# Transformer layer, attention heads: queries projected with their weights stationary and rotated transposed; keys and values token by token, two tiles to a PSUM bank

## The reference

```
h = rms_norm(x);  z = h @ w_in            # columns: pool | q1|q2 | k1|k2 | v | gates
q, k: 8 heads x (2 x 64); rotary on the first 16 of each 64;  v: 8 heads x 128
attn = (softmax(q1 k1) - lambda softmax(q2 k2)) @ v   # block-causal mask by chunks of 64
```

## Time and profile before

| | us |
|---|---|
| median of three runs (845.28 to 847.25) | 845.69 |
| span of the profiled execution | 843.6 |
| heads: from the first projection to the last | 120 to 338 |

### The profile page before, as it was taken

One profiled execution on the slowest core, in us unless ns is written; L12 is line 12 of the kernel. 1 busy time (PEld: TensorE's weight loads), 2 busy tenths in 40 slices (PEclk: granted clock), 3 DMA queues, 4 the chain that ended last, 5 costly groups with the idle time before them and its releaser, 6 DMA issues.

```text
span 843.6 us, 15839 instructions
## 1 busy us (share of the span) xinstructions
PE 821.1 (97%) x5378; PEld 748.1 (89%) x5378; DVE 588.7 (70%) x957; ACT 512.7 (61%) x935; POOL 87.6 (10%) x76
## 2 busy tenths in 40 slices
PE   8999999999999999999999999999999999999992
PEld 7999999999999999999999888888888888888881
DVE  6373332777677768467467126999989999989995
ACT  7343313666566656565525233488888887888884
POOL 0000000000000000000000001222223322223112
PEclk9999999999999999999999999999999999999996
DMA  9632213232133213332234746699999999999925
GB/s 274 139 103 83 67 44 95 82 109 75 36 104 107 59 54 108 102 101 75 79 123 157 270 177 204 236 371 372 380 377 374 368 368 367 364 368 367 351 70 193
DMA packets 135959, 163.54 MB, mean 194 GB/s; under 512 B 18599, under 2 KB 103719, under 8 KB 135914
## 3 DMA queue, kind: packets, MB, share of 16 engines
q1 hardware_dynamic: 129674, 149.53, 52.7%
q0 software_dynamic: 5952, 12.82, 5.4%
q10 hardware_dynamic: 288, 0.59, 0.2%
HBM read 151.61 MB, written 20.12 MB: 204 GB/s over the span
## 4 chain that ended last, share of the span: by engine, by line
PE 52%; DVE 3%; DMA 2%; issue 1%; ACT 1%; POOLq 0%; POOL 0%; ACTq 0%
PE ps L1748 15%; PE ps L1750 15%; PE ps L1749 15%; PE ps L2182 2%; PE ps L2094 1%; DMA xg<-sum_rows,idi 1%; PE ps L2101 1%; PE ps L2204 1%; DMA sum_rows<-yb,ydn 1%; PE ps L2086 0%; PE ps L2127 0%; PE ps L2128 0%; PE ps L2025 0%; DVE wl L1144 0%; PE ps L1953 0%
## 5 line engine op out<-in xcount | busy, mean ns | idle before, releaser
L1623 DVE TENSOR_TENSOR wl<-rawM,wh 128x1024 fp32r<-128x1024 f32 x189 | 223.9, 1220 | 14.3 <-ACT wh L980 12.4
L980 ACT ACTIVATE wh<-rawM 128x1024 fp32r<-128x1024 f32 x192 | 195.8, 1057 | 6.2 <-PE ps L1750 2.8
L1748 PE MATMUL ps<-hTh,wh 128*128 128x272 f32 (+2 forms) x448 | 131.0, 292 | 1.4 <-ACT qkv L804 1.0
L1750 PE MATMUL ps<-hTh,wl 128*128 128x272 f32 (+2 forms) x448 | 129.5, 289 | 0.0
L1749 PE MATMUL ps<-hTl,wh 128*128 128x272 f32 (+2 forms) x448 | 128.9, 288 | 0.0
L1748 PE MATMUL ps<-wh,xh 128*128 128x256 f32 (+1 forms) x384 | 124.3, 324 | 0.3 <-DVE xl L1669 0.3
L1750 PE MATMUL ps<-wh,xl 128*128 128x256 f32 (+1 forms) x384 | 121.7, 317 | 0.0
L1749 PE MATMUL ps<-wl,xh 128*128 128x256 f32 (+1 forms) x384 | 121.6, 317 | 0.0
L1748 PE MATMUL ps<-wh,hTh 128*128 128x384 f32 x256 | 90.0, 352 | 0.2 <-DVE mA L1254 0.2
L1748 PEld LDWEIGHTS ps<-hTh,wh 128*128 128x128 f32 x448 | 84.3, 188 | 3.0 <-ACT qkv L804 1.3
L1750 PE MATMUL ps<-wh,hTl 128*128 128x384 f32 x256 | 86.3, 337 | 0.0
(11 more groups left out here) (324 smaller groups left out, 1711.5 us busy)
## 6 DMA issues: line engine op xcount, KB each, us to landing
rawM<-in_w_expert_up SPq DMA_DIRECT2D x64, 512.0 KB, 9.2
rawM<-in_w_expert_down SPq DMA_DIRECT2D x64, 512.0 KB, 8.0
rawM<-in_w_expert_gate SPq DMA_DIRECT2D x64, 512.0 KB
rawA<-in_w_in SPq DMA_DIRECT2D x64, 192.0 KB, 3.0
rawA<-in_w_in SPq DMA_DIRECT2D x20, 512.0 KB, 5.3
rawA<-in_w_attn_branch SPq DMA_DIRECT2D x8, 512.0 KB, 3.5
rawA<-in_w_out SPq DMA_DIRECT2D x8, 512.0 KB, 4.2
x<-in_x_prompt SPq DMA_DIRECT2D x4, 512.0 KB, 6.7
```

Source lines behind the costliest of these rows:

```text
L980: nc.scalar.activation(wh[:, (c + 1) % S, :], rawM[:, slot, :], ACT.Copy).then_inc(m_hi, 1)
L1623: V.tensor_tensor(wl[:, sl, :], rawM[:, slot, :], wh[:, sl, :].bitcast(F32), ALU.subtract).then_inc(m_lo, 1)
L1748: T.matmul(out, sh, mh_, start=start, stop=False, **kw)
L1750: return T.matmul(out, sl, mh_, start=False, stop=stop, **kw)
```

## The change

Queries are no longer part of the token-by-token projection. For each step j a new `queries(j, half)` holds the 128 query columns of the weights stationary and streams 272 tokens past them, twice, into banks 3 and 4: the queries come out transposed. Keys and values keep their form, with 256 streamed columns instead of 384; tiles 0 and 1 share bank 0, tiles 2 and 3 bank 1, tile 4 has bank 2. So ACT evacuates three times (512, 512 and 256 columns) instead of five (384 each), and `acc_mm` is given after tiles 1 and 3. In steps 0 to 6 the queries come after the tiles, in step 7 ahead of them.

DVE rotates the queries in the transposed layout: `read_queries` multiplies both banks by a table of cosines and swaps the halves by a stream shuffle, `turn_queries` multiplies by a table of sines and adds. Both tables (128 x 544) are loaded once. `turn` makes six transposes (keys only), and the high part of the queries is made from SBUF.

```diff
             def evacuate(h, banks=range(NEV)):
+                for b in banks:
+                    if b < 2:
+                        act.wait_ge(acc_mm, 2 * h + b + 1)
...
             def attend(g, nxt, early=None, last=False):      # ACT
-                act.wait_ge(acc_ev, NT * (g + 1))
+                act.wait_ge(q_done, g + 1)
+                nc.scalar.activation(qh[:], q_turned[:], ACT.Copy).then_inc(q_hi, 1)
+                act.wait_ge(acc_ev, NEV * (g + 1))
...
             def join_sample(g):
-                dve.wait_ge(acc_ev, NT * (g + 1))
-                V.tensor_tensor(qkv[LAST:P, 4, :], ps[2 * DEC:LAST, 4, 0:384], qkv[LAST:P, 4, :],
+                dve.wait_ge(acc_ev, NEV * (g + 1))
+                V.tensor_tensor(kv[LAST:P, 4, :], ps[2 * DEC:LAST, 2, 0:KV], kv[LAST:P, 4, :],
                                 ALU.add).then_inc(dec_done, 1)
+            def read_queries(g, lk):
+                dve.wait_ge(q_mm, g + 1)
+                V.tensor_tensor(two(q_turned[:]), halves, two(q_cos[:]), ALU.mult)
+                V.stream_shuffle(two(q_swap[:]), halves, HALF_SWAP).then_inc(q_free, 1)
+            def turn_queries(g, lk):
+                dve.wait_ge(q_free, g + 1)
+                lk(V.tensor_tensor(q_swap[:], q_swap[:], q_sin[:], ALU.mult))
+                V.tensor_tensor(q_turned[:], q_turned[:], q_swap[:], ALU.add).then_inc(q_done, 1)
...
             def attend(g, nxt, lk, last=False):              # DVE
+                dve.wait_ge(q_hi, g + 1)
+                V.tensor_tensor(ql[:], q_turned[:], qh[:].bitcast(F32), ALU.subtract)
                 dve.wait_ge(tr_hi, 2 * g + 1)
-                V.tensor_tensor(ql[:, 0:SEQ], ps[:, 5, :], qh[:, 0:SEQ].bitcast(F32), ALU.subtract)
...
             DVE's pass, head(h)
+                read_queries(h - 1, lk)
                 if not first:
                     probs(h - 2, 2, lk)
+                turn_queries(h - 1, lk)
                 join_sample(h - 1)
+                rope(h - 1, lk)
                 if not first:
                     probs_lo(h - 2, 2)
-                rope(h - 1, lk)
...
             def project(h, j, after={}):
+                if j == KD - 1:
+                    queries(j, 0, sl, q0)
+                    queries(j, 1, sl, q0).then_inc(q_mm, 1)
                 for t in range(NT):
-                    if j == 0:
-                        pe.wait_ge(acc_ev, NT * (h - 1) + t + 1)
+                    if j == 0 and t % 2 == 0:
+                        pe.wait_ge(acc_ev, NEV * (h - 1) + t // 2 + 1)
                         if t == 4:
                             pe.wait_ge(dec_done, h)
+                    ins = keys_values(j, t, sl, q0)
+                    if j == KD - 1 and t in (1, 3):
+                        ins.then_inc(acc_mm, 1)
...
+                if j < KD - 1:
+                    if j == 0:
+                        pe.wait_ge(q_free, h)
+                    queries(j, 0, sl, q0)
+                    ins = queries(j, 1, sl, q0)
...
             def gate_block(b, after={}):
-                if b < 2:
-                    pe.wait_ge(acc_ev, NT * (HEADS - 1) + 2 * b + 2)
+                if b == 0:
+                    pe.wait_ge(acc_ev, NEV * (HEADS - 1) + 2)
```

More of the change, by code:

```diff
@@ L71 @@
 RA, S, RM = 4, 4, 24
-C_ID, C_COS, C_SIN, C_INV, C_TRI, C_ONE = 0, 128, 288, 448, 508, 636
+C_ID, C_COS, C_SIN, C_INV, C_TRI, C_ONE = 0, 128, 208, 288, 348, 476
 C_IOTA, C_VAL, C_LIST, C_STEP, C_TILE, C_NONE, C_SLOT, C_W = (
-    764, 780, 785, 795, 799, 805, 806, 934)
+    604, 620, 625, 635, 639, 645, 646, 774)
+C_QCOS, C_QSIN, C_ALL = C_W, C_W + TOK, C_W + 2 * TOK
+KV = 2 * P
+HALF_SWAP = [8 + i for i in range(8)] + list(range(8)) + list(range(16, 32))
 def constants():
-    c = np.zeros((P, C_W), np.float32)
+    c = np.zeros((P, C_ALL), np.float32)
     c[:, C_ID:C_ID + P] = np.eye(P)
@@ L87, in constants @@
     for col, f in ((C_COS, np.cos), (C_SIN, np.sin)):
-        t = np.broadcast_to(f(ang)[:, :, None, :], (NT, P, 4, ROT // 2)).transpose(1, 0, 2, 3)
-        c[:, col:col + 160] = t.reshape(P, 160)
+        t = np.broadcast_to(f(ang)[:, :, None, :], (NT, P, 2, ROT // 2)).transpose(1, 0, 2, 3)
+        c[:, col:col + 80] = t.reshape(P, 80)
+    turned = np.concatenate([ang[:4].reshape(SEQ, ROT // 2), ang[4, LAST:]]).T
+    c[:, C_QCOS:C_QCOS + TOK] = 1.0
+    for m in range(2):
+        for half, sign in ((0, -1.0), (1, 1.0)):
+            r = slice(HD * m + ROT // 2 * half, HD * m + ROT // 2 * (half + 1))
+            c[r, C_QCOS:C_QCOS + TOK] = np.cos(turned)
+            c[r, C_QSIN:C_QSIN + TOK] = np.float32(sign) * np.sin(turned)
     for g, w in enumerate(WINDOWS):
@@ L233, in build @@
         gate = at("gate", 170 * K, [P, KD, TOK])
+        q_turned, q_swap, q_cos, q_sin = (at(n, 170 * K + 4 * TOK * b, [P, TOK]) for n, b in (
+            ("q_turned", 4), ("q_swap", 5), ("q_cos", 6), ("q_sin", 7)))
         rawA = at("rawA", 187 * K, [P, RA, SLOT])
@@ L270, in build @@
         acc_rows = nc.dram_tensor("sum_rows", [TOK, D], F32, kind="Internal").ap()
-        id_in, cst_in, w_small, x_in = sem("id_in"), sem("cst_in"), sem("w_small"), [sem(f"x_in{t}") for t in range(NT)]
+        id_in, cst_in, w_small, rows_in = sem("id_in"), sem("cst_in"), sem("w_small"), [sem(f"rows_in{t}") for t in range(NT)]
         raw_in = [sem(f"raw_in{i}") for i in range(RA)]
@@ L309, in build @@
         eps_added = sem("eps_added")
-        fy_in = [sem(f"fy_in{i}") for i in range(NT)]
+        SUMS_IN = [32] * 4 + [48]
         f_out, f_rt, f_done = (sem(n) for n in ("f_out", "f_root", "f_done"))
@@ L791, in hi_head, with evacuate @@
                 nc.scalar.activation(wh[:, sl, 0:w], rawA[:, sl, 0:w], ACT.Copy).then_inc(hi_done, 1)
[L793 to L797, removed]
+            def evacuate(h, banks=range(NEV)):
+                for b in banks:
+                    if b < 2:
+                        act.wait_ge(acc_mm, 2 * h + b + 1)
                     else:
                         act.wait_ge(mm_done, H0 + 4 * h + 4)
-                    if t == 0 and not (isinstance(h, int) and h == 0):
+                    if b == 0 and not (isinstance(h, int) and h == 0):
                         act.wait_ge(kv_out, 64 * h)
@@ L911, in head @@
                        early=lambda: evacuate(h, (0,)))
-                evacuate(h, range(1, NT))
+                evacuate(h, range(1, NEV))
             head(1)
@@ L1383, in _ @@
             split[0] = GB0 + 2
+            read_queries(HEADS - 1, link)
             probs(HEADS - 2, 2, link)
+            turn_queries(HEADS - 1, link)
             join_sample(HEADS - 1)
+            rope(HEADS - 1, link)
             probs_lo(HEADS - 2, 2)
-            rope(HEADS - 1, link)
             split_to(GB0 + 2)
@@ L1856, in _, with queries, keys_values @@
                     ins.then_inc(mm_done if i else pl_mm, 1)
-            def project_first():
[L1860 to L1867, removed]
+            def queries(j, half, sl, q0):
+                tc = slice(HALF * half, HALF * (half + 1))
+                return three(ps[:, 3 + half, 0:HALF], wh[:, sl, q0:q0 + P], wl[:, sl, q0:q0 + P], hTh[:, j, tc], hTl[:, j, tc],
+                             j == 0, j == KD - 1)
+            def keys_values(j, t, sl, q0):
+                wc, first = slice(q0 + P, q0 + 3 * P), j == 0 and t % 2 == 0
+                if t < 4:
+                    return three(kv_bank(t), hTh[:, j, col(t)], hTl[:, j, col(t)], wh[:, sl, wc], wl[:, sl, wc],
+                                 first, j == KD - 1, skip_group_check=True)
+                both = dec[:, 2 * DEC * j:2 * DEC * j + P]
+                T.matmul(kv_bank(t), both, wh[:, sl, wc], start=first, stop=False)
+                return T.matmul(kv_bank(t), both, wl[:, sl, wc], start=False, stop=j == KD - 1)
+            def project_first():
+                sl = H0 % S
                 pe.wait_ge(lo_done, H0 + 1)
@@ L1871, in project_first @@
                 for j in range(2):
-                    tile(j, NT - 1)
+                    queries(j, 1, sl, 384 * j)
+                pe.wait_ge(pa_half, 1)
                 for t in range(4):
[L1874 to L1877, removed]
                     for j in range(2):
-                        ins = tile(j, t)
+                        keys_values(j, t, sl, 384 * j)
+                pe.wait_ge(ws_dve, len(dve_jobs))
+                for j in range(2):
+                    keys_values(j, NT - 1, sl, 384 * j)
+                for j in range(2):
+                    ins = queries(j, 0, sl, 384 * j)
                 ins.then_inc(mm_done, 1)
@@ L1912, in turn @@
                     pe.wait_ge(exp_done, NGR * g)
-                for m in range(2):
-                    for t in range(4):
-                        ins = T.transpose(ps[:, 5 + m, P * t:P * t + P], qkv[:, t, P * m:P * m + P], id_m)
+                for t in range(4):
+                    ins = T.transpose(ps[:, 6, P * t:P * t + P], kv[:, t, 0:P], id_m)
                 ins.then_inc(tr_mm, 1)
```

(5 more changed lines are left out.)

87 lines of the change are left out of this document (47 added, 40 removed).

## The result

The changed kernel takes 862.27 us (median of 4 runs, 861.86 to 865.07) against 845.95 for the one before: ratio 1.0197, 95% interval 1.0185 to 1.0209. The forecast was 856.2, with a range up to 861. The direction and the place were right, the forecast was 6 us too low. The profiled span is 860.1 us, 16.5 more than before.

What follows compares the result with a forecast made beforehand. PE was taken to bound the kernel. Savings of 10.4 us without added waits, set against pass-boundary and scores waits, came to +10.5 us on the profiled 843.6; on the 845.69 median 856.2 us, range 848 to 861.

Steps and rivals of the forecast that it cites:

- What bounds the kernel, and where the change hurts: PE, busy 97% of the span, sets the pace; the change adds PE waits at pass boundaries, 2.82 us a pass.
- The forecast's margins: Time to spare before the change: 0.43 us for atl, 0.06 for the keys' low part, 0.17 for the join.
- The first wait: At the pass boundary PE waits 0.59 us to start `values`, for the low part atl.
- The second wait: PE waits 2.2 us a pass at tile 4 of step 0, for DVE's join of the sample rows.
- The scores: Before the first scores PE waits 0.5 us for the keys' low part, where it waited 0.06 before.
- What PE's list saves: Projection steps save 0.10 us each, 6.4 for 64; five fewer transposes a head save 4.0; together 10.4 us.
- its rival: No narrower pace: 256-column matmuls run as slowly as 272, 11.6 us more, 867 us, half of it 861; chance 0.06.
- a kernel in which all waits are covered: Faster rival: DVE reaches the join in time; with no added waits at all 835 us; chance 0.10.
- The clock: Rival: PE's six stalls each cost a 2.3 us step at half speed, +14 us, 870 us; chance 0.04.
- The sum: Six full passes +11.8 us, head 1 -0.95, head 0 -0.80, last `turn` -0.5, gate +0.9: together +10.5 us.
- The small terms: Among others, `turn`'s five fewer transposes save 0.5 us a head, and the gate's wait adds 0.9 us.
- The gate: After head 7, `gate_block(0)` waits for the copy of bank 1: PE idle 1.9 us instead of 1.0.

Runs made afterwards that it cites:

- the last order: Changed kernel, reordered only: step 7's queries behind tiles 0 and 1, DVE's join ahead of the shuffle, ACT's queries copy ahead of outputs; 841.65 us.

## Why the prediction was wrong, step by step

- **What bounds the kernel, and where the change hurts**: right. PE's list, six pass boundaries, the join behind the queries' rotation. The forecast's margins (0.43, 0.06 and 0.17 us) were the ones that gave way.
- **The first wait**: forecast 0.59 of delay; the start of `values` lies 230.26 - 229.66 = 0.60 behind the last matmul, 0.48 more than an interval. Right within 0.1.
- **The second wait**: 2.2 forecast; 234.61 - 232.24 = 2.37 from start to start, 2.25 more than an interval. The shuffle, taken at 0.69, took 0.78 with the next operation 0.67 behind it, within 0.05 us of the estimate. Both waits together 2.73, forecast 2.82. The Trainium skill's price ("VectorE: DVE Perf Modes", section "The perf-mode tier table"), 0.64 us and up by estimate, agrees with the 0.78 measured.
- **The scores**: 0.5 forecast, 0.43 of idling in most passes. Right, and with its cause: moving ACT's copy of the queries removed it. The last head's scores, which the sum left out, waited 0.7.
- **What PE's list saves: the failed step.** "I take 0.113, the row of the same shape with the same kind of operands." It is 0.118 to 0.120. A step of the projection costs 14 x 0.1185 + 6 x 0.126 = 2.42 us, not 2.34; the 0.10 saved a step became 0.02, for 64 steps 5 us. With 0.1185 in the sum the forecast would have been about 861, and with the 1.5 us of the clock about 862.6. The experts' row does have the width and the roles right, weights streamed past stationary tokens. But other rows of the same trace spoke against it. The heads' own interval, scaled, gives 0.174 x 256 / 384 = 0.116, the one at 272 columns 0.126 x 256 / 272 = 0.1186, and the gate has the width itself (there the tokens stream and the weights are stationary):

```profile
402.83 0.28 PE L1748 MATMUL ps<-hTh,wh 128*128 128x256 f32 x1
...
404.13 0.28 PE L1750 MATMUL ps<-hTh,wl 128*128 128x256 f32 x1
```

(404.13 - 402.83) / 11 = 0.118. One width had two intervals in one trace, and the sum took the shorter as certain. The upper bound was in the working, and its rival had a chance of 0.06. Half of it was put at 861, but 856.2 plus half of 11.6 is 862.0, close to the 862.3 measured, of which 1.5 is the clock's.

- **The same step without the waits**: the prediction has 835 for a kernel in which all waits are covered. With the last order no wait of the loop is left, and it takes 841.65. Its pass is 28.54 - 27.87 = 0.67 shorter than before, where 0.80 + 0.50 = 1.30 was counted: the missing 0.63 is 8 steps at 0.08.
- **The clock**: listed as a rival against the likeliest case at full speed. It was neither: a fall behind one stall of six here, two, five in others. The one in the profile adds 1.5 us. The mechanism named was right, its all-or-nothing form wrong, and its price of 2.3 us too high for stalls of this length. The Trainium skill's warning ("TensorE: Matmul & The Clock Gate", section "HAM oscillation — how this bites in real kernels") and the traces agree that recurring waits can throttle the clock anew, 0.57 of the clock over 4 us; but its example has this in every round, where these runs had it behind 13 of 42 stalls of about 2 us.
- **The sum**: 10.5 + 5 + 1.5 = 17.0 against 16.5 on the profiled span. The rest is small terms of both signs: the waits of a pass were 0.1 shorter and the gate's 0.3, the first pass had no wait of the scores, the last head's scores had one.
- **The small terms**: five transposes fewer saved their 0.5 us a head (the block takes 240.04 - 239.47 = 0.57 instead of 1.11). The gate idled 1.6 us, forecast 1.9.

## What to carry to other kernels

Ahead of a change that adds work to an engine with time to spare, follow that engine's list to the next operation that the bounding engine waits for, and compare the work put in front of it with the time that was to spare there. That DVE was idle for 30% of the span said nothing of this; the 0.17 us ahead of the join did. An order found that way turned 2% slower into 0.5% faster here, with the same instructions. Check the interval of a matmul against more than one row: of the same width in other stages, and of the same stage scaled from other widths. Where they disagree, as 0.113 and 0.118 did here, the sum needs both; 5% of an interval was 5 us. And price a stall that repeats with more than its own length: stalls of about 2 us cost a fall of the clock in 13 of 42 cases here, 1.5 us each, those of 0.6 and 0.8 none.

## What the runs showed of the hardware that I had not expected

- Repeated stalls of PE: 0.6 to 0.8 us never cost the clock (0 of 6 in each of two kernels), about 2 us cost it sometimes (13 of 42 over seven profiled executions: 1 and 2 of 6 in two executions of the same kernel, 5 of 6 in another with the same stalls), 4.9 us always (6 of 6). Between 0.8 and 1.8 us no repeated stall was measured. Each fall behind a stall of 2 us cost 1.5 us, and the number of falls makes otherwise equal runs differ: where the runs of one kernel lie apart (861.86 to 865.07, 862.17 to 868.37), the mean granted clock is lower in the longest (0.988 against 0.991, 0.983 against 0.991).
- The float32 matmuls of 240 to 384 columns in pooling branch, heads and gate start at intervals of about 0.46 ns a column (0.113, 0.118, 0.126, 0.146, 0.174 us at 240, 256, 272, 320, 384). So a step of 5376 columns in 14 matmuls took 2.44 us and one of 5216 in 20 matmuls takes 2.42: the columns decide, and six more matmuls cost next to nothing. The experts' matmuls of 256 columns are the exception, at 0.113.
- DVE's shuffle of 544 columns from PSUM took 0.78 us, with the next operation 0.67 behind its start: about the price of a product of the same size (0.71, the next 0.64 behind).
